# The last of six merges of a triangular inverse, worked on one 64x64 corner instead of the whole 128x128 matrix

## The reference

```python
def step(S, inp):
    r_t, d_t, k_t, v_t, kk_t, a_t = inp
    sa = jnp.einsum('bhvk,bhk->bhv', S, kk_t)
    S = S * d_t[:, :, None, :] - sa[..., None] * (kk_t * a_t)[:, :, None, :] + v_t[..., None] * k_t[:, :, None, :]
    return S, jnp.einsum('bhvk,bhk->bhv', S, r_t)
...
S, y = lax.scan(step, s0.astype(F32), (tm(r), tm(decay), tm(k), tm(v), tm(kk), tm(a)))
```

## Time and profile before

| what | value |
|---|---|
| time, median of 3 runs | 4198.26 us (4196.84 to 4203.59) |
| the profiled execution: its time | 4218.59 us |
| the profiled execution: its span, first to last instruction | 4216.9 us |
| mean granted TensorE clock | 0.934 of full speed |
| RWKV stage (from 640 to 1285 us): TensorE / VectorE / ScalarE busy | 575.8 / 437.0 / 190.0 us of 645 |
| L1629, L1638 and L1640 in it, x864, x720 and x864 instructions | 136.1, 119.8 and 140.5 us busy |

### The profile page before, as it was taken

One profiled execution on the slowest core, in us unless ns is written; L12 is line 12 of the kernel. 1 busy time (PEld: TensorE's weight loads), 2 busy tenths in 40 slices (PEclk: granted clock), 3 DMA queues, 4 the chain that ended last, 5 costly groups with the idle time before them and its releaser, 6 DMA issues. The chain is left out here.

```text
span 4216.9 us, 65548 instructions
## 1 busy us (share of the span) xinstructions
PE 3688.4 (87%) x22444; PEld 3399.8 (81%) x22444; DVE 3269.5 (78%) x6462; ACT 1164.8 (28%) x2127; POOL 1247.5 (30%) x1049
## 2 busy tenths in 40 slices
PE   7997849888995878846769999999999999999997
PEld 6987727777784745526759999999999999999996
DVE  6442646676663269998968999999999999999998
ACT  3101333233221112217962222222222222222221
POOL 1121000000000000000006565565555556555563
PEclk9998768899997989878989999999999999999998
DMA  4785230000003010012468888888888888888885
GB/s 104 86 80 91 85 98 6 20 30 12 1 9 121 10 35 23 23 39 122 199 233 302 296 288 300 290 297 297 284 302 292 299 295 287 303 287 297 295 294 189
DMA packets 291989, 729.45 MB, mean 173 GB/s; under 512 B 27448, under 2 KB 138760, under 8 KB 290336
## 3 DMA queue, kind: packets, MB, share of 16 engines
q0 software_dynamic: 120448, 431.42, 32.9%
q1 hardware_dynamic: 171424, 296.57, 20.9%
HBM read 650.20 MB, written 77.70 MB: 173 GB/s over the span
## 5 line engine op out<-in xcount | busy, mean ns | idle before, releaser
L2566 POOL DMA_INDIRECT experts_u_row<-in_up_rows,experts_u_at x384 | 565.9, 1474 | 635.1 <-DVE experts_dot L2752 517.1
L107 PE MATMUL experts_up_ps<-experts_u_hi,experts_up_hi 128*128 128x352 f32 x2048 | 661.8, 323 | 27.3 <-DVE experts_u_lo L2728 24.8
L107 PE MATMUL experts_down_ps<-experts_act_hi,experts_down_hi 128*128 128x352 f32 x2048 | 676.1, 330 | 9.5 <-DVE experts_down_lo L2728 7.5
L108 PE MATMUL experts_down_ps<-experts_act_lo,experts_down_hi 128*128 128x352 f32 x2048 | 661.0, 323 | 0.0
L108 PE MATMUL experts_up_ps<-experts_u_lo,experts_up_hi 128*128 128x352 f32 x2048 | 660.5, 323 | 0.0
L109 PE MATMUL experts_up_ps<-experts_u_hi,experts_up_lo 128*128 128x352 f32 x2048 | 660.3, 322 | 0.0
L109 PE MATMUL experts_down_ps<-experts_act_hi,experts_down_lo 128*128 128x352 f32 x2048 | 660.2, 322 | 0.0
L2573 POOL DMA_INDIRECT experts_v_row<-in_down,experts_v_at x384 | 514.9, 1341 | 225.7 <-issue 109.2
L2752 DVE CUSTOM_DVE_ANT_0 experts_u_row<-experts_u_row,stream_u_rows_of 128x1024 f32<-128x1024 f32 x384 | 468.2, 1220 | 62.7 <-DMA experts_u_row<-in_up_rows,experts_u_at 62.6
L2765 DVE SCALAR_TENSOR_TENSOR stream_h_rows_of<-experts_v_row,experts_weight,stream_h_rows_of 128x1024 f32<-128x1024 f32 x384 | 497.5, 1296 | 16.1 <-DVE experts_weight L2757 7.3
L2771 DVE TENSOR_TENSOR stream_h<-stream_h,experts_down_ps 128x704 f32<-128x704 f32 x512 | 452.2, 883 | 74.4 <-PE experts_down_ps L109 72.1
(11 more groups left out here) (387 smaller groups left out, 6541.2 us busy)
## 6 DMA issues: line engine op xcount, KB each, us to landing
experts_up<-in_up SPq DMA_DIRECT2D x128, 512.0 KB
experts_down<-in_down SPq DMA_DIRECT2D x128, 512.0 KB
gates<-spread_spread SPq DMA_DIRECT2D x11, 4096.0 KB
experts_gates<-gates SPq DMA_DIRECT2D x64, 704.0 KB
cols<-inp_done POOLq DMA_DIRECT2D x27, 576.0 KB
inp_w_in<-in_w_in SPq DMA_DIRECT2D x27, 512.0 KB
pick_w_query<-in_w_query SPq DMA_DIRECT2D x16, 512.0 KB, 4.1
experts_u_row<-in_up_rows,experts_u_at POOLq DMA_INDIRECT x384
```

Source lines behind the costliest of these rows:

```text
L107: pe.matmul(out, w_hi, x_hi, start=start, stop=False)
L108: pe.matmul(out, w_hi, x_lo, start=False, stop=False)
L2566: pool.indirect_dma_start(u_row[b][:], None, up_rows_d, bass.IndirectOffsetOnAxis(ap=u_at[slot][:, b, a:a + 1], axis=0)).then_inc(u_row_lo ...
```

## The change

In merge 6 the only part of X that is not zero is its lower left 64x64 corner: `join` has entries only in its upper right corner, and `inv` in its upper left block feeds them. The change writes all three steps of merge 6, in every group, for that corner alone. The product X takes the first 64 rows of both operands and 64 columns of each, and its result goes to partitions 64 to 127. ScalarE copies 64 partitions and 64 columns per matrix. The second product takes rows 64 to 127 and gives partitions 0 to 63. VectorE adds 64 partitions. Merges 1 to 5 stay as they are, and every engine has the same instructions in the same order, with the same waits.

```diff
+FIRST, SECOND = slice(0, P // 2), slice(P // 2, P)
...
 # ScalarE
-                        act.activation(neg_x[:, w * group.n:(w + 1) * group.n, :], x_half(w, group.n), ACT.Copy, scale=-1.0).then_inc(x_ready, 1)
+                        rows, cols = (slice(0, P), slice(0, P)) if l < LEVELS - 1 else (SECOND, FIRST)
+                        act.activation(neg_x[rows, w * group.n:(w + 1) * group.n, cols], x_half(w, group.n)[rows, :, cols], ACT.Copy,
+                                       scale=-1.0).then_inc(x_ready, 1)
...
 # VectorE
+                        else:
+                            t = inv_t[FIRST, of_half, SECOND]
+                            dve.tensor_tensor(t, t, z_half(w, 1, n)[FIRST, :, :], ALU.add).then_inc(merged, 1)
...
 # TensorE, the first product
-                            mm = pe.matmul(x_half(w, n)[:, i, :], join[:, w * n + i, :], inv[:, w * n + i, :], start=True, stop=True)
+                            if l < LEVELS - 1:
+                                mm = pe.matmul(x_half(w, n)[:, i, :], join[:, w * n + i, :], inv[:, w * n + i, :], start=True, stop=True)
+                            else:
+                                mm = pe.matmul(x_half(w, n)[SECOND, i, FIRST], join[FIRST, w * n + i, SECOND], inv[FIRST, w * n + i, FIRST], start=True, stop=True)
...
 # TensorE, the second product
-                            mm = pe.matmul(z_half(w, 1, n)[:, i - w * n, :], neg_x[:, i, :], half_cols(inv_t[:, i:i + 1, :], l, 1)[:, 0], start=True, stop=True)
+                            if l < LEVELS - 1:
+                                mm = pe.matmul(z_half(w, 1, n)[:, i - w * n, :], neg_x[:, i, :], half_cols(inv_t[:, i:i + 1, :], l, 1)[:, 0], start=True, stop=True)
+                            else:
+                                mm = pe.matmul(z_half(w, 1, n)[FIRST, i - w * n, :], neg_x[SECOND, i, FIRST], inv_t[SECOND, i, SECOND], start=True, stop=True)
```

More of the change, by code:

```diff
@@ L1413, in merge @@
                             dve.tensor_tensor(t, t, pieces[0], ALU.add)
-                        t = half_cols(inv_t[:, of_half, :], l, 1)
-                        dve.tensor_tensor(t, t, pieces[1], ALU.add).then_inc(merged, 1)
+                            t = half_cols(inv_t[:, of_half, :], l, 1)
+                            dve.tensor_tensor(t, t, pieces[1], ALU.add).then_inc(merged, 1)
+                        else:
+                            t = inv_t[FIRST, of_half, SECOND]
+                            dve.tensor_tensor(t, t, z_half(w, 1, n)[FIRST, :, :], ALU.add).then_inc(merged, 1)
                     at_point(l - 0.5)
```

## The result

| | before | changed |
|---|---|---|
| median of 9 runs each | 4198.26 us (4193.64 to 4210.48) | 4228.59 us (4213.55 to 4240.27) |
| ratio, 95% interval | | 1.0065 [1.0047, 1.0083] |
| profiled execution: its time (span) | 4218.59 (4216.9) us | 4233.56 (4232.0) us |
| mean granted clock of its span | 0.934 | 0.919 |

The kernel is slower by 27 us, outside the range of the prediction. The time stands in the recurrence. I measure it from the first product of merge 1 to the last operation on `rwkv_y` of the last pair. The next two fences give that stretch as one row of busy time by stretch, with the columns of the earlier trace rows. The first is of the kernel before.

The account below looks back on a forecast made before the run. VectorE was taken to bound merge 6's hand-over in 13 of 20 groups. Savings of 0 + 0.1 + 0.5 + 0.35 = 0.95 us took the median of 4198.26 to 4197.3 us, range 4190 to 4205.

Parts of the forecast that it names:

- the 13 groups: Groups where TensorE finishes merge 6 and waits 0.68 to 5.03 us for VectorE's add; forecast gain nothing.
- the tied ones: Group 2 of pairs 0 to 2, VectorE and TensorE tied at merge 6's end; forecast gain 0.03 us each, 0.1 in all.
- The loads' pace: Products of merge 6: 0.056 us per instruction forecast for 0.111, so 0.88 us less in a group of four matrices.
- the copies: ScalarE's copies in merge 6: each of the 32 in the large groups forecast to lose 0.1 us.
- the adds: VectorE's adds in merge 6 on 64 partitions: forecast 0.28 us as now, at best 0.07 us shorter.
- line 1607: Follows merge 6 in group 4 of pairs 0 to 2; forecast 0.16 us earlier each, 0.5 in all, limited by line 1342.
- The sum of 0.95 us: Whole forecast saving: 0 + 0.1 + 0.5 + 0.35 us, between a gain of 1.5 and a loss of 2.2.
- the third rival: Longer rests at merge 6's hand-over make TensorE's clock fall more often; three stretches give 4211 us; chance 0.07 slower.
- the groups 3: Part of the argument against the clock falling more often: in three groups 3 a fall comes anyway within 3 us.
- The bounds of the range: 4190 to 4205 us, from mechanism, spread of the runs shown, and one clock stretch of 4.6 us more or less.
- The signs of being wrong: Wait for line 1415 doesn't grow; first add to merge 1 changes from 0.43 us; stage clock moves 0.01 or more.
- Theory G: Changes of operand shape around merge 6 cost the path; forecast as dear gaps, 4200.5 us at 0.21 us each, chance 0.02.

Follow-up runs that it names:

- products: Kernel before with both products of merge 6 and the add on the corner, ScalarE's copy whole; ratio to before 1.0067.
- twice: Changed kernel with each 64x64 product of merge 6 issued two times; ratio to before 1.0010.
- half_whole: Kernel before with only the first of each two products issued in merge 6 of the large groups, shapes whole; ratio to before 1.0050.
- warm_before: Kernel before with 222 spare products added where TensorE rests longest for VectorE in the recurrence; ratio to before 0.9923.
- rest_filled: Changed kernel with spare whole products behind merge 6, 4 in groups 0, 1 and 3, 2 in group 2, none in group 4; ratio to before 1.0024.
- narrow: Kernel before with copy and add on the corner, first product of merge 6 with whole weights but 64 columns, second whole; ratio to before 1.0007.

## Why the prediction was wrong

- **That nothing of the saving lies on the path in the 13 groups, and next to nothing in the tied ones: right.** VectorE's first add still stands 0.42 us ahead of merge 1. The loads' pace (0.056 us), the copies (0.1 us less) and the adds (no change worth counting) came as worked out. So did line 1607: it started 0.22 us behind the end of the bonus add of line 1342 (800.91 to 801.13), and now starts 0.05 behind it (784.01 to 784.06), 0.17 us earlier for the forecast 0.16.
- **The sum of 0.95 us: right as far as its terms go, and beside the point.** A term was missing. In the 13 groups I wrote "nothing: TensorE gets to its wait earlier and waits longer". Waiting longer had a price.
- **The step that failed is the weighing of the third rival.** I named the mechanism and gave it 0.07, with the argument that a fall comes anyway in the groups 3 and "elsewhere dense work follows at once". Both halves failed. In group 3 the fall came earlier, 0.9 us behind the start of merge 6 for the former 7.7, and the stretch was 17 us and not 10. And in group 4, which I had left out because TensorE hardly rests there, it fell between dense stretches. I looked only for long rests, and took those rests' lengths one at a time. The runs with one product each show that the time saved counts, not the place.
- **The price was mis-sized too.** I counted two more stretches as the point from which it decides, and three as the bad case. There were nine more falls and 146 us more at the lower clock in the two profiled executions (95 us over all runs of `products`). The rival's own number, 4211, was still 17 us too low. (Small slips in its sums: three stretches at 4.6 us are 13.8 and give 4212, two fewer give 4189, and the row of 770 to 771 puts the fall at 770.7, not 770.9.)
- **The bounds of the range** took one stretch more or less. All 20 groups have the same shape of work, four pairs over, so what tips in one tips in its sisters: the falls in merge 6 of groups 3 and 4 stand in pairs 0, 1 and 2 alike. A chance spread over independent places was the wrong picture.
- **The signs of being wrong that I had named** did show: the wait for VectorE's adds fell from 31.7 to 26.3 us instead of growing to 38, and the stage's clock moved by 0.10, ten times the mark. The third, the distance from VectorE's first add to merge 1, stayed.
- **Theory G** was priced in the right order: the gaps hold at most the 0.1% of `twice`, 0.2% at the end of its interval.

## What to carry to other kernels

On an engine whose granted clock moves in the trace, taking work off it where another engine sets the pace need not be free: look at the granted clock around the place, at the short rests together with the long ones, and multiply by how often the place repeats. Where the clock dips in such a stage, try the reverse, cheap products that nobody reads in the waits; here 222 of them gained 0.8% and the removal of useless work lost 0.65%.

## What the runs showed of the hardware

- TensorE's granted clock, two levels only (1.00 and 0.50, 2.4 and 1.2 GHz), fell at 784.6 though in the 20 us before it no product had waited for another engine for more than 0.31 us (no weight load for more than 0.49). The Trainium skill, TensorE: Matmul & The Clock Gate, Part 1, says that the clock follows how busy TensorE has been of late. The traces agree in sign where work was taken off TensorE (0.82 in the changed kernel, 0.85 in `half_whole`, for 0.92 before) and where it was added in the waits (0.97 in `warm_before`; 0.87 in `rest_filled` for 0.82).
- The clock also fell with TensorE at work as long as before: with whole weight loads and half the result columns in one product of merge 6 it was 0.9278 over the ten executions of `narrow` (0.925 to 0.930), for 0.9319 over twenty of before (0.929 to 0.935).
- Each of the two instructions of a float32 product with a stationary operand of 64 rows by 64 columns and 64 result columns issues 0.056 us behind the one before, half the 0.111 of a whole one.
- A float32 add on 64 partitions takes VectorE 0.273 us, on 128 partitions 0.281; a copy out of PSUM takes ScalarE 0.271 us for 64x128 and 0.280 for 128x128. The number of partitions hardly counts.
